# Input projections of two token blocks on one read of weights, rings of eight rows, weights read where they lie

## The reference

```python
h = rmsnorm(x, norm_mix)
x = x + hybrid_mixer(h, ...)           # h @ w_in (1024 x 2152) splits into the inputs of three branches:
                                       # latent attention, a gated linear recurrence, differential attention;
                                       # their outputs, normalized and joined, go through w_out
h = rmsnorm(x, norm_cross)
x = x + memory_cross_attention(h, rmsnorm(mem, norm_mem), w_cq, w_ckv, w_co)
h = rmsnorm(x, norm_ffn)
x = x + peer_ffn(h, peer_w_q, peer_keys, peer_u, peer_v)
return rmsnorm(x, norm_final)

def peer_ffn(h, w_q, keys, u, v):      # for each token: 8 heads x 16 experts, out of 16384
    experts, g = ...                   # top 16 of 128 keys on two sides, top 16 of their sums, softmax
    act = gelu(einsum('td,thkd->thk', h, u[experts]))
    return einsum('thk,thkd->td', g * act, v[experts])
```

## Time and profile before

| | |
|---|---|
| median of 3 runs | 3485.63 us (3483.43 to 3486.24) |
| the profiled execution: span from the first to the last instruction | 3488.4 us |
| its time beside the span | the profile lists nothing outside of the span |
| bytes that DMA moved | 1345.09 MB |
| gathers of u and v rows | 2048 of 512 KB |
| loads of pairs of weights | 408 of 512 KB, and 49 copies |

### The profile page before, as it was taken

How to read it: one execution, slowest core, us unless ns; L and a number is a source line. 1 busy time by engine, 2 the same in 40 slices (tenths; PEclk the granted TensorE clock), 3 DMA queues, 4 the chain that set the end, 5 groups by cost and what they waited for, 6 DMA issues and landing times.

```text
span 3488.4 us, 34790 instructions
## 1 busy us (share of the span) xinstructions
PE 2948.9 (85%) x10984; PEld 1651.9 (47%) x10984; DVE 2349.6 (67%) x5893; ACT 812.5 (23%) x1915; POOL 2015.7 (58%) x2085
## 2 busy tenths in 40 slices
PE   7876898888988898889997899888998889976675
PEld 6465455544545355534554456444564445522222
DVE  6229846886588765886578765886648865596555
ACT  3111411132211421133211322114221232211111
POOL 1004755666566765666565655665556655477775
PEclk9898999999999999999999999998999999999998
DMA  7788999999999999999999999999999999999998
GB/s 279 277 274 313 408 409 409 408 409 409 409 407 406 394 409 409 408 407 382 409 409 408 392 356 409 409 409 348 359 409 409 409 355 342 385 404 410 409 409 347
DMA packets 386971, 1345.09 MB, mean 386 GB/s; under 512 B 41762, under 2 KB 44834, under 8 KB 386148
## 3 DMA queue, kind: packets, MB, share of 16 engines
q0 software_dynamic: 294912, 1073.87, 78.1%
q1 hardware_dynamic: 90724, 264.79, 20.0%
q10 hardware_dynamic: 1152, 4.19, 0.3%
HBM read 1332.99 MB, written 35.39 MB: 392 GB/s over the span
## 4 chain that ended last, share of the span: by engine, by line
PE 38%; DMA 30%; DVE 15%; POOL 9%; issue 6%; ACT 3%; SPq 1%; DVEq 0%; POOLq 0%; ACTq 0%
PE ps_sum L1267 18%; DMA rows<-in_peer_u,ids_u 13%; DMA rows<-in_peer_v,ids_v 10%; PE ps_p L999 5%; POOL rows L824 5%; POOL rows L810 4%; DVE rows L2052 4%; PE ps_s L1181 4%; DMA rows<-in_peer_v,ids_u 3%; DMA w_ring<-packed 3%; PE ps_s L1118 2%; PE ps_p L1126 2%; DVE feat_b L1935 1%; DVE feat_b L1931 1%; PE ps_s L1114 1%
## 5 line engine op out<-in xcount | busy, mean ns | idle before, releaser
L1267 PE MATMUL ps_sum<-rows,diag 128*128 128x512 f32 x3548 | 1727.6, 629 | 267.1 <-DMA rows<-in_peer_v,ids_v 141.4
L2052 DVE CUSTOM_DVE_ANT_0 rows<-h_cur,rows 128x1024 f32<-128x1024 f32 x1024 | 1226.8, 1220 | 496.3 <-DMA rows<-in_peer_u,ids_u 483.3
L810 POOL DMA_INDIRECT rows<-in_peer_u,ids_u x1024 | 1012.3, 989 | 702.0 <-issue 483.3
L1267 PEld LDWEIGHTS ps_sum<-rows,diag 128*128 128x128 f32 x3548 | 671.0, 200 | 1155.7 <-issue 1005.7
L824 POOL DMA_INDIRECT rows<-in_peer_v,ids_v x512 | 490.3, 958 | 433.8 <-PE ps_sum L1267 277.6
L824 POOL DMA_INDIRECT rows<-in_peer_v,ids_u x512 | 498.2, 973 | 284.7 <-PE ps_sum L1267 144.2
L1528 ACT ACTIVATE diag<-ident,acts 128x128 f32<-128x128 f32 x887 | 324.7, 394 | 1049.4 <-PE ps_sum L1267 750.1
L999 PE MATMUL ps_p<-hT,w_ring 128*128 128x128 f32 x2944 | 358.7, 282 | 28.8 <-DMA w_ring<-packed 15.3
L999 PEld LDWEIGHTS ps_p<-hT,w_ring 128*128 128x128 f32 x2944 | 353.0, 198 | 61.2 <-issue 39.7
L1834 DVE CUSTOM_DVE_ANT_0 e<-ps_s,bias_t 128x256 f32<-128x256 f32 (+6 forms) x96 | 74.2, 773 | 176.3 <-PE ps_s L1118 73.7
L2074 DVE SCALAR_TENSOR_TENSOR x_cur<-rows,acts,x_cur 128x1024 f32<-128x1024 f32 x137 | 175.6, 1282 | 7.4 <-DMA rows<-in_peer_v,ids_v 7.3
(11 more groups left out here) (288 smaller groups left out, 2376.2 us busy)
## 6 DMA issues: line engine op xcount, KB each, us to landing
w_ring<-packed SPq DMA_DIRECT2D x343, 512.0 KB
w_ring<-in_wstream SPq DMA_DIRECT2D x65, 512.0 KB
packed<-in_wstream SPq DMA_DIRECT2D x49, 512.0 KB, 8.2
rows<-in_peer_u,ids_u POOLq DMA_INDIRECT x1024, 14.9
rows<-in_peer_v,ids_u POOLq DMA_INDIRECT x512, 12.6
rows<-in_peer_v,ids_v POOLq DMA_INDIRECT x512, 19.3
bias_rows<-rows SPq DMA_DIRECT2D x5, 1024.0 KB, 12.1
bias_t<-in_x SPq DMA_DIRECT2D x8, 512.0 KB, 7.9
```

Of the source, the lines that this page charges most:

```text
L810: pool.indirect_dma_start(u_rows[:, slot, :], None, peer_u, bass.IndirectOffsetOnAxis(ap=ids_u[:, j:j + 1], axis=0)).then_inc(u_landed[slo ...
L1267: ins = pe.matmul(ps_sum[:, c * 512:(c + 1) * 512], diag[:, n % 4, :], v_rows[:, slot, c * 512:(c + 1) * 512], start=(j == 0), stop=(n == ...
L2052: dve.tensor_tensor_reduce(row, h_cur[:, :], row, 1.0, 0.0, ALU.mult, ALU.add, dots[:, p:p + 1]).then_inc(u_used, 1)
```

## The change

Nothing of what is computed changes. Its parts:

- **Two blocks on one read.** Bodies 1, 3 and 5 (`TWICE`) make the input projections of blocks b+1 and b+2 together: each pair of weights is used for the first block and then for the second. Bodies 2, 4 and 6 make none and load none; they only load what comes first in the next body (`only_ahead`). The second block's inputs (a second load of x, at `load_later_x`) are normed after the first's; its sums go into the banks of `ps_s`, its results into new buffers. As `ps_s` is taken, the spreading of the ffn gain for `hand_ids` moves behind the last tile of `next_4` in these bodies. `TENSOR_STOPS` is unchanged; `SCALAR_STOPS` gets a `next_3`.
- **Rings of 8 rows** for u and v; the two rows of 4 KB per partition make room for the new buffers.
- **Weights read in place.** `packed` and its copies go. A partition reads two consecutive rows of one slice, a run of 4 KB. That permutes the contraction index, so the activations are permuted alike: `as_read` is the order of `x_next`, of the scaled x and of the memory, and the per-column gains are loaded in that order by 13 small DMAs that ACT issues. Four pairs of w_out per block (`WHOLE`) keep runs of 2 KB. A tile of 128 columns now holds columns of both halves of a row, so the two row products turn both halves after both are added.
- DVE's waits on running counts (`wait_more`, a register) become waits on constants.

```diff
-U_RING = 9
-V_RING = 9
+U_RING = 8
+V_RING = 8
+WHOLE = [IN_SLICES + n * KT + kt for n in range(2) for kt in (2, 4)]
+TWICE = (1, 3, 5)
+def lane(b):
+    return int(b - 2 in TWICE)
+def heads(b):
+    return (b + 1, b + 2) if b in TWICE else (b + 1,)
+def prepares(b):
+    return b == 0 or b in TWICE
...
+        in_banks = [[ps_p[g][:, :], ps_s[:, g * HALF:(g + 1) * HALF]] for g in range(2)]
+        xs_in, later_hT = (x_in, bias_t[:, 0, :]), xs[:, :].rearrange("p (a t) -> p a t", a=KT)
+        def as_given(t):
+            return t[:, :].rearrange("p (h k q s) -> p h k q s", h=2, k=4, s=2)
+        def as_read(t):
+            return t[:, :].rearrange("p (s k h q) -> p h k q s", h=2, k=4, s=2)
...
             def load_pair(i, n):
                 ge(sp, w_used, n - 2 * W_RING + 2)
-                    src = packed[(i - MEM_SLICES) // 2]
+                dst, src = w_ring[:, slot_of(n), :], wstream[i:i + 2]
+                if i - MEM_SLICES in WHOLE:
+                    dst, src = dst.rearrange("p (s c) -> p s c", s=2), src.rearrange("s p c -> p s c")
...
+                else:
+                    src = src.rearrange("h (q s) c -> (h q) (s c)", s=2)
                 sp.dma_start(dst, src).then_inc(w_landed[slot_of(n)], 16)
-            def pack(first, last):
-                for i in range(first, last):
-                    src = wstream[MEM_SLICES + 2 * i:MEM_SLICES + 2 * i + 2].rearrange("s p c -> p s c")
-                    sp.dma_start(packed[i].rearrange("p (s c) -> p s c", s=2), src)\
...
+            def load_later_x(b):
+                sp.wait_ge(bias_used, (b - 1) * (DIFF_H + 1))
+                sp.dma_start(xs_in[1], x[bass.ds(b * P, P), :]).then_inc(x_early[1], 16)
+            def only_ahead(b):
+                load_rope(b + 1)
+                load_bias(b + 1, DIFF_H)
+                front_loads(b + 1, per_tile * 17, per_tile * 17 + ahead_slices)
...
             def opening(p):
-                    pack(i - 1, i + 1)
...
-            def project(b, g, first, n):
+            def project(blocks, g, first, n):
+                b = blocks[0]
                 for i in range(n):
                     pace.part(i / n)
...
+                    for half in range(2):
+                        w = block_slice(b, 2 * (first + i) + half).rearrange("p (k c) -> p k c", k=4)
+                        for own in blocks:
+                            lhs, dst = (hT[:, :, :], later_hT)[lane(own)], in_banks[g % 2][lane(own)][:, i * P:(i + 1) * P]
                             for k in range(4):
                                 kt = 4 * half + k
+                                sides = (w[:, k, :], lhs[:, kt, :]) if g < 4 else (lhs[:, kt, :], w[:, k, :])
+                                ins = pe.matmul(dst, *sides, start=(kt == 0), stop=(kt == KT - 1), skip_group_check=True)
+                        ins.then_inc(w_used, 1)
...
             def later_norm(b):
-                spread_ffn(b)
+                if b == 0:
+                    spread_ffn(b)
                 turn_scaled(b + 1)
+                if b in TWICE:
+                    pe.wait_ge(k_out, 2 * b + 2)
+                    turn_in(b + 2)
+            def next_project_4(b):
+                project(heads(b), 4, 15, 2)
+                if b in TWICE:
+                    for g in (3, 4):
+                        pe.wait_ge(proj_out[g][1], nth(b + 2) + 1)
+                    spread_ffn(b)
...
-            def row_product(b, first, lhs, norm, made, count):
+            def row_product(b, first, lhs, made, count):
-                        if n == 1 and kt == 4:
-                            turn_added(b, norm, 0)
...
             def norm(b, n):
                 pace.part(0.6)
-                turn_added(b, n, 1)
+                for g in range(2):
+                    turn_added(b, n, g)
...
             def first_norm():
+                load_gains()
                 square_x(0, 0)
...
+            def next_norm(b):
+                scale_x(b + 1)
+                pace.part(0.7)
+                gain_in(b + 1)
+                if b in TWICE:
+                    scale_x(b + 2)
+                    gain_in(b + 2)
...
-                dve.scalar_tensor_tensor(h_cur[:, :], x_next[:, :], small[:, 105:106], ps_s[:, :], ALU.mult, ALU.mult)\
+                for n in range(2):
+                    for half in range(2):
+                        ins = dve.scalar_tensor_tensor(as_given(h_cur)[:, n, :, :, half], as_read(x_next)[:, n, :, :, half],
+                                                       small[:, 105:106], as_given(ps_s)[:, n, :, :, half], ALU.mult, ALU.mult)
```

More of the change, by code:

```diff
@@ L93, with nth @@
 FRONT_END = EXPERTS
+TWICE = (1, 3, 5)
+def lane(b):
+    return int(b - 2 in TWICE)
+def nth(b):
+    return sum(lane(n) == lane(b) for n in range(b))
+def heads(b):
+    return (b + 1, b + 2) if b in TWICE else (b + 1,)
+def prepares(b):
+    return b == 0 or b in TWICE
 def on_vector(b, j):
@@ L543, in counter, with stages @@
             return reg
-        def stages(front, last=False):
-            return {n: f for n, f in front.items() if n not in FIRST_STAGES and not (last and n in NEXT_STAGES)}
+        def stages(front, b):
+            return {n: f for n, f in front.items() if n not in FIRST_STAGES and not (n in NEXT_STAGES and not prepares(b))}
         def row_of(bp, p, lag):
@@ L681, in load_bias @@
                     ge(sp, bias_used, b * (DIFF_H + 1) + max(turn - 1, 0))
+                if turn == 0 and b - 1 in TWICE:
+                    sp.wait_ge(scaled[1], nth(b + 1) + 1)
                 keys_n = P * (key_tiles(b) if turn else mask_tiles[0])
@@ L768, in _ @@
                     front["cross_q"] = lambda b: front_loads(b, per_tile * 25, per_tile * 33)
+                only = {} if prepares(first) or first == NB - 1 else {"next_4": only_ahead}
                 with sp.Fori(first, last) as b:
-                    pace.run(stages(front, last=first == NB - 1), b)
+                    pace.run(stages(front, first) | only, b)
             sp.wait_ge(fin_stored, 16 * NB)
@@ L1296, in _ @@
                     front["mla_up"] = later_up
-                if first == NB - 1:
+                if not prepares(first):
                     front["peer_scores"] = last_scores
+                elif first in TWICE:
+                    front["peer_scores"] = peer_scores
                 with pe.Fori(first, last) as b:
                     pace.start(b - 1)
-                    pace.run(stages(front, last=first == NB - 1), b)
+                    pace.run(stages(front, first), b)
             pace.start(NB - 1)
@@ L1559, in _ @@
                               "project_1": lambda b: second_project(), "project_4": lambda b: first_exps()}, 0)
-            front["latents"] = project_3
             for pace.body, (first, last, wide[0]) in enumerate(LOOPS):
+                for name, stage, here in (("latents", project_3, lane(first) == 0),
+                                          ("next_3", lambda b: later_project_3(b + 2), first in TWICE)):
+                    if here:
+                        front[name] = stage
+                    elif name in front:
+                        del front[name]
                 with act.Fori(first, last) as b:
                     pace.start(b - 1)
-                    pace.run(stages(front, last=first == NB - 1), b)
+                    pace.run(stages(front, first), b)
             pace.start(NB - 1)
```

367 lines of the change are left out of this document (218 added, 149 removed), and 8 rows, old and new, of the table SCALAR_STOPS.

## The result

The changed kernel took 3516.76 us (median of 4 runs, 3511.29 to 3523.38) against 3485.18 us of the kernel before beside it: a ratio of 1.0097, 95% interval 1.0078 to 1.0115. That is 0.97% slower, where 3472 was predicted, in a range of 3430 to 3507.

The account below looks back on a forecast made before the run. The prediction took the loops to be bound by DMA bytes, with short interludes bound by PE. Its terms, -57 + 24 + 3.9 + 15.4 - 1.3 + 1.6 = -13.4 us, gave 3472 us, range 3430 to 3507.

Parts of the forecast that it names:

- What hides most of it is the DMA queue: Odd tails: some 24 us of queued transfers land during PE's 25.5 us lateness, leaving 3.8 us dry.
- work added to the tails of bodies 1, 3 and 5: Second block's projections make PE 25.5 us late; 8 us lost per odd body, bounds 3 and 25.5, sum +24.
- a dry gap that begins before position 121: Sign that the forecast is wrong: DMA in the odd tails runs dry already before position 121.
- rival (a): Odd tails, positions 99 to 128: POOL's order drains the queue, each costs the whole 25.5 us; 3525, chance 0.21.
- extra load of x: Bodies 1, 3 and 5: one more load of x each, 3 x 1.28 = +3.9 us, where DMA is full.
- Loads removed, -57: Bodies 2, 4 and 6 load no input weights: 19 us saved each, bounds 12 and 21.8, sum -57.
- Rings of 8, +15.4: Six late-body attention stretches where DMA runs dry do so 2 rows earlier: +15.4 us, bounds 0 and about 30.
- Block 0, -1.3: Block 0's start: no weight copies -4.0, later turns +1.4, gain loads 0, one gathered row fewer +1.3; together -1.3 us.
- Read in place, split and strided operations, +1.6: Four weight pairs per block in 2 KB runs: +1.6 us; split and strided operations 0, bounds 0 and +8.
- (b): Whole loop: all bytes count, odd tails fully hidden, even ones save all 21.8 us; -61, 3424, chance 0.19.
- (c): Odd tails cost about 12 us each, it cancels, and the time stays within 7 us of 3485; chance 0.14.
- (d): Even tails: POOL's issue is the limit, 16 us saved per even body, not 19; 3481, chance 0.06.

Follow-up runs that it names:

- rings_8: The kernel before with u and v rings of 8 rows in place of 9, nothing else changed: 3500.05 us, 1.0048.
- even_tiles: The changed kernel with only PE's tile stops changed in bodies 1, 3 and 5, double tiles standing singly over positions 104 to 127: 3506.54 us, 1.0066.
- one_sum: The changed kernel with 7 of 8 of the second block's projection products skipped in bodies 1, 3 and 5, output not kept right: 3468.22 us, 0.9972.
- late_gain: The kernel before, unpaired, rings of 9; in bodies 1 to 6 PE spreads the ffn gain behind next_4, twelve times: 3645.76 us, 1.0462.
- one_by_one: The changed kernel with no paired bodies, each body projecting its own next block, rings of 8 kept: 3503.37 us, 1.0055.
- rings_7: The kernel before with u and v rings of 7 rows in place of 9, nothing else changed: 3522.56 us, 1.0107.

## Why the prediction was wrong

**The failed step is "What hides most of it is the DMA queue"** in the work added to the tails of bodies 1, 3 and 5. What stands ahead of it held: the list of PE's work, 25.5 us late, and the chain from the last tile over the spreading and ACT's copies to h_cur. Counted from block 0's first product, h_cur of body 1 came 29.8 us later than before, 5.1 of them ahead of position 93 and 24.7 in the tail; PE's 131.88 us of work and its two waits of 2.96 and 7.01 are 141.85, where the list had 142.5. The step then took 21.7 us off for transfers in the queue, which left 3.8 us dry, and 5 more for the restart. By the stretches above DMA lost 144 x (1 - 377/409) = 11.3 us in this tail and 25 x (1 - 268/409) = 8.6 behind it, some 20 in all; before it lost next to nothing in its tail (408 GB/s). The step was wrong in two ways.

First, the queue was not there. From 650 to 692 us landings fell from 24 to 25 us before to 21 in rings_8 and 7.8 after (10 in the stretch of the earlier trace rows), for POOL, which issues u and v rows in one order, stands at a v row whenever PE's sums are late (42.0 us in this tail). PE was late from the first norm on, at 600 us, so the queue, short at that point in all three (12.7 us to landing from 575 to 600 us before, 9.3 in rings_8, 7.4 after), did not grow again in the 100 us before h_cur was due. The sentence "a dry gap that begins before position 121" named this as a sign. It is rival (a)'s mechanism, though not the group of seven double tiles keeps the queue short but the sum of PE's work: in even_tiles, without the groups, landings stay at 6.1 and 7.6 us, and in one_sum, without most of the work, they are back at 20.3 and 20.7.

Second, even a full queue covers little (late_gain: 4 to 9 of 33.6 us). Rows that land during a stall are a gain only if the engine that uses them is then faster than DMA brings rows. DVE, with the front end's first stages between its products (busy for 23.28 of the 25 us from 725 on), took 20.6 us over 8 positions with the rows ready; DMA needs 8 x 2.56 = 20.5. So most of the stall stays lost: about 20 of the 29.8 us here.

The term then was +24 for the three bodies and is +60.1 against one_by_one, with the extra load of x in it, which was counted at +3.9 apart. Per body the tail has +21.4, and with the 8 positions behind it +18.1, under rival (a)'s 25.5, and its 3525 is nearer to 3517 than the forecast.

The other terms, as signed there:

- *Loads removed, -57.* The even bodies are 51.6 us shorter, 17 each for 19, inside of the bounds. But only 11 of the 17 lie in the tail (117.0 to 106.0), where DVE is busy for 96.55 of 105 us and DMA is at 1.01. Of the rest 3.4 lie in the first 8 positions (24.0 to 20.6), where the rows that landed in the odd tail's stall lie ready; that isn't this term's. With the 8 positions behind it, read in the same way, an even tail is 14.0 us shorter.
- *Rings of 8, +15.4.* +17 (1.0048), and +20 for the next pair of rows. The size is right; that it is lost in the six dry stretches isn't shown (2.5 of 5.3 us in rings_8's execution, 13.6 of 33.3 in that of rings_7), so the match is in part luck.
- *Block 0, -1.3.* The six kernels with the gains first start the first product 1.3 us later on the mean than the four with before's block 0 (306.5). That isn't told from nothing, as single executions differ by about 7. The sum is near by luck, since its parts are not: the gains were costed at 0 under DVE's wait at 17.70 us and cost some 6.5, because the chain runs over x's square and PE's first tiles, not over the square of the memory rows; all else is worth about 5, not 1.3.
- *Read in place, split and strided operations, +1.6.* Not told from nothing: 0.0007 between one_by_one and rings_8, block 0 included.

By these, with 2.5 us for the 0.0007, 60.1 - 51.6 + 17 + 2.5 = +28; the ratio gives 34 (27 to 40). Of the rivals, (b) and (c) are out with the odd tails; (d), POOL's pace in the even ones, was not tried by itself.

## What to carry to other kernels

Batching two uses of one load moves the work of two into one stretch: add up each engine's list in that stretch alone before the bytes are counted as saved, and if an engine comes out late there, take most of its lateness as lost (here about 20 of 29.8 us, in late_gain 24 of 33.6). A queue of transfers was little of a cushion: the consumer could not afterwards run faster than the transfers, and the lateness itself kept the queue short. A wait of the late engine was worth its full length some 110 us ahead of the end, and moving the result that others wait for mostly moved where it is paid.

## What the hardware showed that was not expected

In late_gain PE did 48 matmul instructions with a contraction of one row, one behind the other, in 36.83 us; four of these took 1.95 us after, so 23.4 were expected. PE's granted clock in the stretch from 700 to 725 us is 0.50, the lower of its two levels, 1.2 GHz, while PE was busy for 25.00 of 25 us; before the fall PE did tiles and sums with 128 rows, and the stretch with both has 0.77. The Trainium skill, page "TensorE: Matmul & The Clock Gate", section "Why this matters for your kernels", names idle gaps between bursts of matmuls as what brings the clock down in mid-kernel. The trace after agrees with it at the wait of 7.01 us (0.51 from 605 to 615 us, with PE busy for 2.99 of 10). In late_gain it fell in a stretch without a gap; whether the one row did it was not tried apart.
